# Gate and up projections of two feed-forward layers: seven block products for eight, with the weight sums on GpSimd

## What is computed

```python
h = rms_norm(x, g_pre);  x = x + 0.5 * rms_norm((silu(h @ w_gate) * (h @ w_up)) @ w_down, g_post)   # FFN 1
h = rms_norm(x, g);      proj = h @ w_in        # mixing: 8-head stick-breaking attention,
...                                             # 4-head retention, gates, two projections, merge
x = x + rms_norm(merged @ w_out, g)
h = rms_norm(x, g_pre);  x = x + 0.5 * rms_norm((silu(h @ w_gate) * (h @ w_up)) @ w_down, g_post)   # FFN 2
```

## Time and profile before

| | |
|---|---|
| median of three runs | 1491.92 us |
| the profiled execution, its own time | 1491.14 us |
| its span, first to last instruction | 1489.4 us |
| TensorE busy (matmuls) | 1458.0 us, 98% of the span |
| VectorE, ScalarE, GpSimd busy | 573.5, 494.0, 55.1 us |
| mean granted TensorE clock | 0.997 |

### The profile page before, as it was taken

One profiled execution on the slowest core, in us unless ns is written; L12 is line 12 of the kernel. 1 busy time (PEld: TensorE's weight loads), 2 busy tenths in 40 slices (PEclk: granted clock), 3 DMA queues, 4 the chain that ended last, 5 costly groups with the idle time before them and its releaser, 6 DMA issues.

```text
span 1489.4 us, 17867 instructions
## 1 busy us (share of the span) xinstructions
PE 1458.0 (98%) x6680; PEld 1197.4 (80%) x6680; DVE 573.5 (39%) x664; ACT 494.0 (33%) x735; POOL 55.1 (4%) x116
## 2 busy tenths in 40 slices
PE   6999999999999999999989999999999999999997
PEld 6888888888888878767768888888888888888886
DVE  4322222223333373656764343632222222233334
ACT  4222222222222252557764323522222222232222
POOL 0000000000000000332320000000000000000000
PEclk9999999999999999999999999999999999999999
DMA  7333333332322333211112345233333333332221
GB/s 233 99 99 99 99 99 87 98 97 99 113 99 98 118 101 121 71 57 59 56 36 85 92 157 167 71 85 99 98 98 87 98 97 99 99 113 97 89 97 57
DMA packets 195474, 145.97 MB, mean 98 GB/s; under 512 B 4592, under 2 KB 180976, under 8 KB 195312
## 3 DMA queue, kind: packets, MB, share of 16 engines
q1 hardware_dynamic: 194432, 142.10, 31.3%
q10 hardware_dynamic: 1008, 3.41, 0.6%
HBM read 141.30 MB, written 4.19 MB: 98 GB/s over the span
## 4 chain that ended last, share of the span: by engine, by line
PE 92%; DVE 5%; ACT 2%; POOL 1%; issue 0%; DMA 0%; ACTq 0%; DVEq 0%; POOLq 0%
PE ps L421 21%; PE ps L422 20%; PE ps L423 20%; PE ps L428 9%; PE ps L430 9%; PE ps L429 9%; PE ps L646 1%; DVE w_lo L1030 1%; DVE ps L1046 1%; DVE x_tok L1049 1%; PE ps L601 1%; PE ps L608 1%; DVE xn L1059 1%; DVE h_lo L1065 0%; DMA g_b<-g_ffn_pre 0%
## 5 line engine op out<-in xcount | busy, mean ns | idle before, releaser
L1030 DVE TENSOR_TENSOR w_lo<-w_raw,w_hi 128x1024 fp32r<-128x1024 f32 (+1 forms) x260 | 309.1, 1191 | 595.7 <-ACT w_hi L756 594.9
L421 PE MATMUL ps<-h_hi,w_hi 128*128 128x512 f32 (+1 forms) x1376 | 529.3, 385 | 4.8 <-DVE h_lo L1065 2.9
L423 PE MATMUL ps<-h_hi,w_lo 128*128 128x512 f32 (+1 forms) x1376 | 522.8, 380 | 0.0
L422 PE MATMUL ps<-h_lo,w_hi 128*128 128x512 f32 (+1 forms) x1376 | 522.5, 380 | 0.0
L756 ACT ACTIVATE w_hi<-w_raw 128x1024 fp32r<-128x1024 f32 (+1 forms) x260 | 260.1, 1028 | 248.5 <-PE ps L430 241.5
L421 PEld LDWEIGHTS ps<-h_hi,w_hi 128*128 128x128 f32 x1376 | 259.6, 189 | 63.8 <-issue 11.6
L422 PEld LDWEIGHTS ps<-h_lo,w_hi 128*128 128x128 f32 x1376 | 259.6, 189 | 49.5 <-issue 1.9
L423 PEld LDWEIGHTS ps<-h_hi,w_lo 128*128 128x128 f32 x1376 | 259.5, 189 | 49.3
L798 ACT ACTIVATE gate_s<-ps 128x512 f32<-128x512 f32 x64 | 38.4, 599 | 514.7 <-PE ps L423 514.7
L428 PE MATMUL ps<-w_hi,a_hi 128*128 128x512 f32 x512 | 199.4, 390 | 0.9 <-DVE a_lo L1084 0.9
L430 PE MATMUL ps<-w_hi,a_lo 128*128 128x512 f32 x512 | 199.2, 389 | 0.0
(11 more groups left out here) (114 smaller groups left out, 875.8 us busy)
## 6 DMA issues: line engine op xcount, KB each, us to landing
w_raw<-w_ffn_gate SPq DMA_DIRECT2D x64, 512.0 KB, 4.0
w_raw<-w_ffn_up SPq DMA_DIRECT2D x64, 512.0 KB, 4.0
w_raw<-w_ffn_down SPq DMA_DIRECT2D x64, 512.0 KB, 3.2
w_raw<-w_in SPq DMA_DIRECT2D x44, 512.0 KB, 3.8
w_raw<-w_out SPq DMA_DIRECT2D x8, 512.0 KB, 5.5
x_mid<-x_tok SPq DMA_DIRECT2D x4, 512.0 KB, 8.2
w_raw<-w_proj_sb SPq DMA_DIRECT2D x8, 256.0 KB, 2.6
w_raw<-w_proj_ret SPq DMA_DIRECT2D x8, 256.0 KB, 2.5
```

What stands on the lines that cost most here:

```text
L421: pe.matmul(ps[:, bank, out_cols], wh, src_hi, start=first, stop=False)
L422: pe.matmul(ps[:, bank, out_cols], wh, src_lo, start=False, stop=False)
L423: return pe.matmul(ps[:, bank, out_cols], wl, src_hi, start=False, stop=last)
L1030: dve.tensor_tensor(w_lo[:, slot, 0:cols], w_raw[:, slot, 0:cols], w_hi[:, slot, 0:cols].bitcast(F32), ALU.subtract).then_inc(w_lo_done, 1)
```

## The change

Gate/up of a pair p of column blocks (256 gate columns and 256 up columns, 16 pairs in an FFN) is one 2x2 block product. The stream is cut into token halves (FIRST, SECOND) and channel halves, the weights into four blocks of 512 channels x 256 columns: RAW11 and RAW21 are the gate's upper and lower channels, RAW12 and RAW22 the up's. Before, such a pair took eight block products (4 units of 24 matmuls with 512 columns); now it takes seven, by Winograd's form of Strassen's scheme, each of 24 matmuls with 256 token columns:

- stream sums, once for each FFN, by VectorE from PSUM and a copy `a1` of the first token half: s3, s2, s4, s1 (`stream_sums`), each then split into hi and lo. Product m = 1, 2 uses the plain first half, 4 the plain a22, 3, 5, 6, 7 use s4, s1, s2, s3.
- weight sums, four for each pair, by GpSimd, each a 128x1024 float32 add or subtract from SBUF to SBUF: 7 = RAW22 - RAW12, 6 = sum 7 + RAW11, 4 = RAW21 - sum 6, 5 = RAW12 - RAW11. The sum is written where the lo of that product will be, so it waits for the same product of the pair before to be done.
- hi and lo of seven weight tiles for each pair (before: four).
- three PSUM banks are copied to SBUF by ScalarE (m1, u2, m7), VectorE adds a PSUM bank to each copy, then two silus and two multiplies of 512 columns.
- x_tok's place is used by the sums: FFN 1 reads x again at its down stage, FFN 2 writes x_tok to `x_mid` (`x_left`) and reads it back.

The core of the diff, first GpSimd's `pair`, then SyncE's loads, VectorE's lo, and last TensorE's first products with VectorE's order at the start:

```diff
+            def pair(p, free):
+                    pool.wait_ge(raw_full[RAW12], p * 16 + full)
+                    pool.wait_ge(raw_full[RAW22], p * 16 + full)
+                    pool.wait_ge(unit_done, free(7))
+                    weight_sum(7, raw(RAW22), raw(RAW12), ALU.subtract)
+                    pool.wait_ge(t_pool, p * 4 + (fi * T_POOL + 1))
...
+                    weight_sum(6, t_of(7), raw(RAW11), ALU.add)
+                    pool.wait_ge(t_pool, p * 4 + (fi * T_POOL + 2))
...
+                    pool.wait_ge(w_lo_done, p * PRODUCTS + (u0 + 2))
+                    pool.wait_ge(unit_done, free(4))
+                    weight_sum(4, raw(RAW21), t_of(6), ALU.subtract)
+                    pool.wait_ge(unit_done, free(5))
+                    weight_sum(5, raw(RAW12), raw(RAW11), ALU.subtract)
```

```diff
+                def pair(p):
+                    fetch(RAW11, block(RAW11, p), (t_pool, p * 4 + fi * T_POOL))
+                    fetch(RAW12, block(RAW12, p))
+                    fetch(RAW21, block(RAW21, p))
+                    fetch(RAW22, block(RAW22, p), (w_lo_done, p * PRODUCTS + u0))
...
+                fetch(RAW22, block(RAW22, 1), (w_lo_done, u0 + splits(0, 3)))
```

```diff
+            def weights_lo(fi, u0, p, m):
+                slot = PLACE[m]
+                dve.wait_ge(w_hi_done, count(u0, p, m, "split"))
+                if m in (1, 2, 3):
+                    whole_w = w_raw[:, {1: RAW11, 2: RAW21, 3: RAW22}[m], :]
+                else:
+                    if m in (6, 7):
+                        dve.wait_ge(t_pool, p * 4 + (fi * T_POOL + {7: 2, 6: 3}[m]))
+                    whole_w = w_sum[slot][:, :]
+                dve.tensor_tensor(w_lo[slot][:, :], whole_w, w_hi[slot][:, :].bitcast(F32), ALU.subtract
+                                  ).then_inc(w_lo_done, 1)
```

```diff
+FIRST_PE = ((0, 1), (0, 2), (1, 1), (1, 2), (0, 6), (0, 7), (0, 5), (0, 4), (0, 3), (1, 6), (1, 7), (1, 5), (1, 4), (1, 3))
...
+            def stream_sums(n, t):
+                made_before = 4 * n + 4 * (t - 2)
+                dve.wait_ge(xt_done, TT * n + t + 1)
+                dve.wait_ge(a1_kept, n + t - 1)
+                dve.tensor_tensor(half(s3, t), a1[:, 0:KH, tok(t - 2)], block_of(t, 0), ALU.subtract).then_inc(comb_done, 1)
...
-            split_u(0)
+            weights_lo(0, U_UP1, 0, 1)
             stream_lo(0, 1)
             normalise(0, 2, G_PRE1)
-            split_u(1)
+            weights_lo(0, U_UP1, 0, 2)
             normalise(0, 3, G_PRE1)
-            stream_lo(0, 2)
-            split_u(2)
-            stream_lo(0, 3)
-            split_u(3)
+            stream_sums(0, 2)
+            early(U_UP1, 1)
+            stream_sums(0, 3)
+            gate_first(U_UP1, 0, 1)
+            early(U_UP1, 2)
             ffn(0, U_UP1)
...
+                comb_lo(fi, 6)
+                weights_lo(fi, u0, 0, 6)
+                comb_lo(fi, 7)
+                weights_lo(fi, u0, 0, 7)
+                gate_first(u0, 1, c0 + 2)
+                weights_lo(fi, u0, 0, 5)
+                comb_lo(fi, 5)
+                weights_lo(fi, u0, 0, 4)
+                comb_lo(fi, 4)
+                comb_lo(fi, 3)
+                up_second(u0, 0, 0, c0 + 4)
+                weights_lo(fi, u0, 0, 3)
+                gate_second(u0, 0)
+                weights_lo(fi, u0, 1, 7)
+                weights_lo(fi, u0, 1, 6)
```

More of the change, by code:

```diff
@@ L324, in gain @@
             def gain(i):
[L326 to L334, removed]
-                    for j in range(SLOTS):
[L336 to L344, removed]
+                sp_eng.dma_start(G_TILE[i], gains[i].unsqueeze(0).broadcast_to([P, D])).then_inc(g_in[i], 16)
@@ new lines, in early, with gate_first @@
+            def early(u0, m):
+                dve.wait_ge(w_hi_done, u0 + splits(1, m))
+                dve.tensor_tensor(early_lo[m][:, :], early_raw[m][:, :], early_hi[m][:, :].bitcast(F32),
+                                  ALU.subtract).then_inc(w_lo_done, 1)
+            def gate_first(u0, p, copies):
+                dve.wait_ge(copied, copies)
+                dve.wait_ge(unit_done, count(u0, p, 2, "made"))
+                dve.tensor_tensor(m1_c[:, :], m1_c[:, :], ps[:, B_M2, :], ALU.add).then_inc(summed, 1)
@@ new lines, in up_second, with gate_second, gated_second @@
+            def up_second(u0, p, par, copies):
+                dve.wait_ge(copied, copies)
+                dve.wait_ge(unit_done, count(u0, p, 5, "made"))
+                dve.tensor_tensor(m7_c[:, :], m7_c[:, :], ps[:, B_UP[par], :], ALU.add).then_inc(summed, 1)
+            def gate_second(u0, p):
+                dve.wait_ge(unit_done, count(u0, p, 4, "made"))
+                dve.tensor_tensor(u2_c[:, :], u2_c[:, :], ps[:, B_DOWN, :], ALU.add).then_inc(summed, 1)
+            def gated_second(p, silus, sums):
+                a = act[:, p, :, SECOND]
+                dve.wait_ge(silu_done, silus)
+                dve.wait_ge(summed, sums)
+                dve.tensor_tensor(a, a, pair_cols(m7_c), ALU.mult).then_inc(a_done, 1)
@@ new lines, in gated_first, with turn_of, part @@
+            def gated_first(u0, p, par, silus):
+                a = act[:, p, :, FIRST]
+                dve.wait_ge(silu_done, silus)
+                dve.wait_ge(unit_done, count(u0, p, 3, "made"))
+                dve.tensor_tensor(a, a, bank_cols(B_UP[par]), ALU.mult).then_inc(a_done, 1)
+            def ffn(fi, u0):
+                ud = u0 + PRODUCTS * NG
+                c0, s0 = 3 * NG * fi, 2 * NG * fi
+                def turn_of(p, par, last=False):
+                    weights_lo(fi, u0, p, 6)
+                    weights_lo(fi, u0, p, 4)
+                    gate_first(u0, p, p * 3 + (c0 + 1))
+                    weights_lo(fi, u0, p, 5)
+                    weights_lo(fi, u0, p, 3)
+                    if not last:
+                        weights_lo(fi, u0, p + 1, 1)
+                        weights_lo(fi, u0, p + 1, 2)
+                    up_second(u0, p, par, p * 3 + (c0 + 3))
+                    if last:
+                        split_u(ud)
+                    gate_second(u0, p)
+                    if last:
+                        part(0)
+                        split_u(ud + 1)
+                    else:
+                        weights_lo(fi, u0, p + 1, 7)
+                    gated_second(p, p * 2 + (s0 + 2), p * 3 + (c0 + 2))
+                    gated_first(u0, p, par, p * 2 + (s0 + 1))
+                def part(f):
@@ L1312, in _ @@
+            weight_sums(0, U_UP1)
             nl = nw = nrope = 0
```

631 lines of the change are left out of this document (487 added, 144 removed).

## The result

| | kernel before | changed kernel |
|---|---|---|
| median, lowest to highest (us) | 1491.57, 1491.22 to 1491.97 | 1502.39, 1502.08 to 1502.65 |
| profiled span (us) | 1489.4 | 1500.4 |
| TensorE busy | 98% | 95% |

The ratio is 1.0072 (95% interval 1.0056 to 1.0088): slower by 0.7%, 10.8 us. The prediction said 1497, with 1487 to 1507 for this forecast.

A forecast was written before the change was run, and what follows sets the result against it. It took a series of GpSimd sums, VectorE remainders and loads (20.75 us a turn) to bound the loop, not TensorE; FFN terms +2.0 and +0.3 plus clock 3.2 gave +5.5, so 1497 us, range 1468 to 1518.

The forecast's parts named there:

- Matmuls: Gate/up on TensorE: 256-column matmuls start 0.120 us apart, 20.16 us a pair, gaining 26.9 us in each FFN.
- A sum alone: GpSimd's 128x1024 weight sum with nothing beside it takes about 2.38 us.
- Exclusion in turns: VectorE's two-SBUF-input work and GpSimd's sums alternate by whole instructions; the one that waits is next.
- Turn 20.75: One loop turn is set by remainders, load and sums: 20.45 or 21.05 us by order, middle 20.75, against TensorE's 20.16.
- clock term: Behind each FFN's hole between pairs 0 and 1, matmuls run at half clock: 1.6 us each, 3.2 together.
- The hole: TensorE waits 11.7 us (8 to 12) between pairs 0 and 1, once in each FFN.
- The start: FFN starts: first product at 17.3 and 963.3 us, (0,5) ending at 48.8 and 987.4, within 4 us each.
- The sum: Whole kernel: down starts +2.0 and +0.3 us, half clock 3.2, together +5.5 on the span, giving 1497 us.
- A: Rival: TensorE bounds the loop turn at 20.16 us; 1482 us, down to 1466 with shorter holes and starts; chance 0.32.
- B: Rival: sum 4 always goes first and waits add 0.5, a loop turn of 21.6 us; 1519 us; chance 0.19.
- C: Rival: each GpSimd sum costs 4.1 us, 7 us more a turn, some 1670 us; chance 0.04 shared with D.
- D: Rival: rewrite fails its purpose, matmul starts 0.13 us or more apart, 27 us more; chance 0.04 shared with C.

The follow-up runs named there:

- experiment 5: Changed kernel with GpSimd's first weight sum of each FFN held until remainders of token tiles 0, 1 and weight block 1 are done: 1502.34 us.
- 4: Changed kernel with sum 5 made by VectorE behind lo6 instead of by GpSimd, from pair 1 on: 1512.76 us.
- experiment 1: Changed kernel with block 3 of the first pair split ahead of up_second, so RAW22 of pair 1 is fetched earlier: 1489.95 us.
- experiment 7: Changed kernel with the edits of experiment 1, experiment 5 and experiment 6 together: 1474.51 us.
- 8: Kernel of experiment 7 with hi and lo of the first pair's block 3 moved ahead of those of block 7: 1473.75 us.
- 9: Kernel of experiment 8 with the first pair's product (0,7) computed ahead of (0,6), its splits moved likewise: 1477.91 us.
- experiment 6: Changed kernel with block 3 split first in the loop and RAW22 loaded ahead of RAW21: 1491.42 us.

## Why the prediction was right, and where it was not

The sign, the size and the mechanism came out. Step by step:

- **Matmuls.** 0.120 us a start, 20.16 a pair. With the loads in the right order the loop ran at 20.26. Right.
- **A sum alone** was put at 2.38, measured 2.34 (56.43 to 58.84 us in the hole, where VectorE rests); beside a remainder 3.2 to 3.4. Right. So the mean of 2.05 of the earlier trace rows had waits in it and was not a price.
- **Exclusion in turns.** Shown by experiment 5 (3.38 against 1.22 at the same start) and by 4. In the steady loop lo7 went first, then sum 4, gated_second, sum 5, lo6, which is the branch priced at 20.45; the issues of RAW22 lie 20.48 apart in the turn shown. The Trainium skill (SBUF — State Buffer, "SBUF: two separate sides") says that the first holds the ports for its whole instruction; by that rule, the trace agrees, and who is next after it the runs show: the one that waits.
- **Turn 20.75.** Steady turns were 20.65 on average. From (1,6) to (15,6) the text and its clock term make 21.4 + 13 x 20.75 + 1.6 = 292.75; measured 292.66 in the first FFN, 289.88 in the second. Right, but partly by luck: I named one closed series and took 0.18 us for the issue and 3.6 for its load; the issue came 0.03 us behind lo3 and the load took 4.1. There are two series, and each is some 20.5 long.
- **The hole,** 11.7: measured 11.65 and 11.99, and the half clock behind it cost 1.7 and 1.5 us, as priced (1.6). Right. What experiment 1 then made of it, that this cost goes with most of the hole, was wrong: holes of 4.1 to 4.9 us in experiments 1, 7, 8 and 9 cost 1.3 to 2.7 us of it. The Trainium skill (TensorE: Matmul & The Clock Gate, "Why this matters for your kernels") warns of such gaps; the rows at 68.84 and 71.40 agree.
- **The start.** E, the end of (0,5), was put at 48.8 and came at 50.6 (68.03 - 11.65 - 5.76). The step that failed is "RAW22 ... lands at about 17.5, and sum7 begins behind the normalise of tile 2": it landed at 16.6, and so sum 7 got the ports ahead of the remainder of tile 1. The first product came at 20.74, not 17.3. Experiment 5 gives 2.2 us of these 3.4 to the sum. The other 1.3 were there without it (18.58), by a second slip: I counted one copy of ScalarE, that of tile 1, but it copies tile 0 before it as well, and hi1 now stands ahead of the hi of tile 0. The remainder of tile 0 on VectorE, before and after:

```profile
12.66 1.22 DVE L1065 TENSOR_TENSOR h_lo<-ps,h_hi 128x1024 fp32r<-128x1024 f32 x1 [1.79 <-ACT h_hi L789]
```

```profile
14.98 1.22 DVE L1410 TENSOR_TENSOR a_lo<-a,a_hi 128x1024 fp32r<-128x1024 f32 x1 [4.16 <-ACT a L1008]
```

Half of the 3.4 was made up by E. With the sums held back E still came at 50.0, so only 0.6 of its 1.8 us hang on the sum beside tile 1; the rest is the later list, not traced further. In the second FFN, counted from the output product, the first product was put at 54.9 and came at 54.2, and E at 79.0 and came at 80.9.

- **The sum.** A plain error: I took the row at 1310.18 for the first down matmul of the second FFN. It is a later one; the stage begins at 1307.46. So "FFN 2: ... +0.3" should have read +3.0, and the total +8.2, 1500 and not 1497. The rest of the 11.0 is the first FFN, by its late E (+1.7), the second FFN (-0.6: E 1.9 and the hole 0.3 later, the loop 2.9 shorter), and 1.7 outside the gate/up stages: 1.2 in mixing and 0.5 in the down stages. The slip made the number smaller, and 1497 fell inside its range all the same.
- **The rivals.** A (the loop bound by TensorE) was not the case, by 0.4 us a turn (20.65 against 20.26), and experiment 6 shows how near it was: one line of the load order. Turns of B's length did occur in front of (3,6) and (4,6) of the first FFN (21.25 and 21.94), not later; why there is open. C and D were not the case.

What I missed altogether is where the time could be had. I took 11.7 us of hole as a consequence of the change, where 7 of them were the place of one instruction in two lists.

## What to carry to other kernels

When a stage is bound by a closed series through several engines, write down every series through the same buffers and price each: shortening one of two equal ones gave 2.7 us here, mending both 11.0. A load's landing time depends on the loads issued just ahead of it (6.4 us behind three of them, 4.1 when they were 3.8 us older). In hand-written lists, the instruction that frees a buffer for the next load belongs as early as its own inputs allow, ahead of work that nobody waits for. A gain in front of a loop that is bound by something else may not arrive at the end; try it again once the loop is mended.

## What the runs showed of the hardware

The lower clock (0.213 us between matmuls of 256 columns) did not last longer behind a longer hole. It lasted 3.8 and 3.2 us behind the holes of 11.65 and 11.99 us of the changed kernel, 5.7 and 4.8 us behind 4.63 and 4.85 in experiment 1, and 3.8 and 2.9 us behind 4.63 and 4.69 in experiment 7. Shortening a hole from 12 to 4.6 us gave back the hole and little or nothing of the clock.

The same two gaps of TensorE in the mixing stage (2.54 and 0.89 us) were followed by stretches at the lower clock of different length. The windows of the kernel before, then of the changed one (us, busy time of five engines with counts, granted clock, DMA share, GB/s):

```profile
766.00:768.00 2.00, 2.00 (x7) 0.51 (x6) 1.97 (x2) 1.97 (x4) 0.00 (x0) 0.62 0.01 2
768.00:770.00 2.00, 2.00 (x10) 1.62 (x10) 1.80 (x5) 1.22 (x3) 0.93 (x2) 1.00 0.00 0
```

```profile
773.00:775.00 2.00, 2.00 (x6) 0.77 (x6) 1.93 (x5) 1.45 (x4) 0.93 (x2) 0.52 0.00 0
775.00:777.00 2.00, 2.00 (x10) 1.64 (x9) 1.04 (x3) 0.48 (x1) 0.00 (x0) 1.00 0.00 0
```

The granted clock was at half from about 764.5 to 767.5 us in the one and from about 768.5 to 774.9 in the other. The changed kernel pays 1.2 us more there, in code that the change does not touch. Of the ten profiled executions that have the changed kernel's mixing stage, two took 362.9 to 363.0 us for it and eight 361.5 to 361.8, with the kernel before at 361.7. So these 1.2 of the 11.0 us come from the clock of the execution in the trace, and not from the work of the change. Whether the other three executions of the changed kernel, up to 0.6 us longer, had them too no trace shows.
